# Up projections with features on partitions, two activation buffers, and modulation sums in pieces: one change to a two-block transformer kernel

## The chip, the cores and the metric

The kernel runs as one program on one core of a Trainium2 chip. A core has a matmul engine (TensorE, PE), three elementwise engines (VectorE or DVE, ScalarE or ACT, GpSimd or POOL), and SyncE (SP), which here only issues transfers from the chip's memory. The metric is the device time of one execution in microseconds (us), lower being better. A kernel's time is the median of its runs. Engines run their own instruction streams in program order and meet only at semaphores: an instruction waits until a counter has reached a value, and adds to a counter when it is done. So what stands ahead of an instruction on its engine delays it, whatever the data allow.

## The reference, cut to what matters

A two-layer block and then a one-layer block run over 256 tokens of 1024 features in float32. The parts that matter here:

```
def squared_relu_mlp(h, w_up, w_down):          # layers 0 and 1: D_FF = 4096
    a = jax.nn.relu(h @ w_up)
    return (a * a) @ w_down

for i in range(2):                              # first block
    mod = silu(c) @ w_mod[i] + b_mod[i]         # 1024 x 6144, a vector for each layer
    sh1, sc1, g1, sh2, sc2, g2 = split(mod, 6)
    y = pool_mixer(...) if i == 0 else moba_attention(...)
    x = x + g1 * y
    h = modulate(rmsnorm(x, norm_mlp[i]), sh2, sc2)
    x = x + g2 * squared_relu_mlp(h, w_up[i], w_down[i])

def swiglu(x, w_gate, w_up, w_down):            # second block: D_FF_2 = 2816
    return (silu(x @ w_gate) * (x @ w_up)) @ w_down
```

The second block has a gated delta rule and an attention with forgetting between its input projection and its SwiGLU; the change doesn't touch them.

## The kernel before, in words

**Precision.** Every large product is made of three passes in float32r: the high part of the weights (`wh`) by the high part of the data (`H`, or `aTh` for the activation), the low part of the weights (`wl`) by the high part of the data, and `wh` by the low part (`L`, `aTl`). The high part of a loaded weight block is a copy made by ScalarE (line 557), the low part a subtraction on VectorE (line 1049).

**Weights.** `raw` has four slots of 2 MB, loaded by SP. `wh` and `wl` hold one weight block at a time, in two halves. A block is called T; `split(T)` is four pieces, two for each half, first on ScalarE (which waits for the load, and for `split_used`, that TensorE has used the same half of the block before), then on VectorE (which waits for ScalarE's piece). TensorE waits with `half(T, hb)` for VectorE's second piece of a half. SP may load a slot again when VectorE has split the block in it (`free_split`).

**An MLP iteration.** Each of the first two MLPs has 8 iterations of 512 hidden features, numbered 0 to 7 and 8 to 15. `up(it)` makes 256 tokens x 512 features, tokens on partitions, in two banks of PSUM: for each half of the weights (4 of the 8 blocks of 128 input features) and each of 2 token blocks, 4 x 3 matmuls of 512 columns, 48 in all. ScalarE takes the relu of it (line 602), POOL squares it (line 452), `turn(it)` transposes it with 8 matmuls against the identity (line 1646) into two more banks, ScalarE copies out the high part `aTh` (line 607), VectorE the low part `aTl` (line 1083), and `down(it)` adds its product with 512 rows of `w_down` into four banks (line 1661, 48 matmuls). TensorE's order is up(0), turn(0), up(1), down(0), turn(1), up(2), down(1), turn(2) and so on: up(j), down(j - 1), turn(j). The T of up(j) in the first MLP is T_MLP0 - 1 + 2j, of down(j) T_MLP0 + 2 + 2j. The SwiGLU stage has 11 iterations of 256 features with the gate's and the up's columns side by side in one block (`g_up`, line 1593), a product on VectorE in place of the square (line 1489), four transposes (`g_turn`, line 2066) and 24 matmuls of `g_down` (line 2077).

**Modulation sums.** The vector `mod` needs 12 blocks of 512 columns for each layer. VectorE multiplies a block's rows by silu(c) and adds them up into `acc` (`mod_sum`, line 909), and TensorE sums over the partitions with one-column matmuls (line 1547, 1712, 1723). During the first MLP this goes on for layer 1: in iterations 2 to 7 a unit of 2 x 256 columns is loaded into slots 0 and 1, `mod_halves(j)` sums it on VectorE in one piece of 16 instructions (lines 933 and 936), TensorE's 8 small matmuls follow down(j - 1), and `mod_cols1(j)` adds the bias to the result in PSUM (line 964). Slots 0 and 1 are loaded again when `mod_halves` is done with them; the last block of `w_down` goes into slot 0 after unit 7. `gate_diag` and `gate_mm` (lines 993 and 1611) spread a gate over the partitions, by 8 small VectorE instructions and 16 matmuls, before the last down projection.

**Query and key projections.** They already have the other layout (line 1749): weights stationary, tokens moving, 256 columns a matmul, features on partitions.

The order of VectorE's work in the first MLP's loop, which the prediction follows:

```
with e.Fori(2, 7) as j:
    split(T_MLP0 + 2 * j, 3)          # down(j - 1)
    mod_halves(j)
    split(T_MLP0 + 1 + 2 * j, 2)      # up(j + 1)
    mod_cols1(j)
    mlp_aT(j)
```

## Time and profile before

| what | value |
|---|---|
| median of 3 runs | 1230.62 us (1228.77 to 1233.9) |
| span of the profiled execution | 1229.1 us |
| mean granted TensorE clock, share of 2.4 GHz | 0.892 |
| TensorE busy | 1098.8 us (89%), 5513 matmuls |
| VectorE busy | 681.5 us (55%) |
| ScalarE busy | 451.5 us (37%) |
| GpSimd busy | 109.6 us (9%) |
| data loaded | 193.76 MB, 159 GB/s over the span |

The span runs from the first to the last instruction of one profiled execution. It is the only time that this execution has of its own; it lies inside the range of the runs, 1.5 us below their median. Busy is time in which an engine had at least one instruction in work. A matmul's row gives a modelled length from its start until its last result (0.39 us for 512 columns), but matmuls are pipelined, so what counts is the distance between the starts of two neighbours. The first MLP lies at 114 to 323 us, the second at 516 to 712, the SwiGLU stage at 1017 to 1219.

### The profile page before, as it was taken

How to read it: one execution, taken by the hardware profiler on the slowest of the kernel's cores; microseconds unless marked ns; L12 is line 12 of the kernel's file. 1: busy time of each engine (PE TensorE's matmuls, PEld its weight loads, DVE VectorE, ACT ScalarE, POOL GpSimd, SP SyncE). 2: the span in 40 equal slices, each digit the busy share in tenths (PEclk: the TensorE clock that was granted, in tenths of full speed). 3: DMA queues.
4: the chain of work that ended last, by engine and by line, in shares of the span. 5: the costliest groups of instructions: out<-in, count | busy, mean ns of one | idle time of the engine just before them, and what ended most of it. 6: DMA issues, size and time to landing. Idle time of an engine off the chain costs nothing.

```text
span 1229.1 us, 14350 instructions
## 1 busy us (share of the span) xinstructions
PE 1098.8 (89%) x5513; PEld 927.8 (75%) x5513; DVE 681.5 (55%) x1074; ACT 451.5 (37%) x748; POOL 109.6 (9%) x108
## 2 busy tenths in 40 slices
PE   5489999999799898899999879999869689999995
PEld 5488777777698688678888669986659677777774
DVE  5487666776645894544444366623373545554453
ACT  1113433433444321444444345542222334443342
POOL 2000100101000000010010010001074000000000
PEclk9976999999799657899999869985679988999998
DMA  9876577677354653154454513540000023545510
GB/s 342 286 271 228 211 253 266 208 270 271 140 206 151 206 192 138 71 200 160 185 196 177 188 47 131 203 137 1 1 1 1 19 85 103 183 159 191 185 68 34
DMA packets 105178, 195.47 MB, mean 159 GB/s; under 512 B 2283, under 2 KB 46572, under 8 KB 105132
## 3 DMA queue, kind: packets, MB, share of 16 engines
q1 hardware_dynamic: 104380, 192.58, 44.6%
q0 software_dynamic: 752, 2.26, 0.5%
q8 instruction: 31, 0.51, 0.2%
q14 instruction: 15, 0.12, 0.0%
HBM read 193.76 MB, written 1.07 MB: 159 GB/s over the span
## 4 chain that ended last, share of the span: by engine, by line
PE 70%; DVE 16%; ACT 5%; issue 5%; DMA 3%; POOL 1%; SPq 1%; DVEq 0%; ACTq 0%; POOLq 0%
PE ps L1593 16%; PE ps L1632 12%; PE ps L1661 10%; PE ps L1858 6%; DVE wl L1049 5%; PE ps L1749 4%; DMA raw<-in_w_mod 3%; PE ps L2077 3%; DVE arena L909 2%; PE ps L1543 2%; ACT wh L557 2%; DVE arena L936 2%; PE ps L1993 1%; ACT arena L574 1%; PE ps L1762 1%
## 5 line engine op out<-in xcount | busy, mean ns | idle before, releaser
L1049 DVE TENSOR_TENSOR wl<-raw,wh 128x1024 fp32r<-128x1024 f32 (+1 forms) x288 | 314.0, 1135 | 306.1 <-ACT wh L557 305.8
L557 ACT ACTIVATE wh<-raw 128x1024 fp32r<-128x1024 f32 (+1 forms) x288 | 267.9, 982 | 364.6 <-PE ps L1593 135.1
L1593 PE MATMUL ps<-wh,H 128*128 128x512 f32 x288 | 117.5, 408 | 6.1 <-DVE L L1032 3.3
L1593 PE MATMUL ps<-wl,H 128*128 128x512 f32 x288 | 116.2, 403 | 0.0
L1593 PE MATMUL ps<-wh,L 128*128 128x512 f32 x288 | 115.4, 401 | 0.0
L1661 PE MATMUL ps<-wh,aTh 128*128 128x512 f32 x256 | 103.2, 403 | 8.9 <-DVE wl L1049 8.9
L1632 PE MATMUL ps<-wh,H 128*128 128x512 f32 x256 | 103.4, 404 | 2.4 <-DVE wl L1049 2.4
L1661 PE MATMUL ps<-wl,aTh 128*128 128x512 f32 x256 | 102.7, 401 | 0.0
L1661 PE MATMUL ps<-wh,aTl 128*128 128x512 f32 x256 | 102.5, 400 | 0.0
L1632 PE MATMUL ps<-wl,H 128*128 128x512 f32 x256 | 101.4, 396 | 0.0
L1632 PE MATMUL ps<-wh,L 128*128 128x512 f32 x256 | 101.2, 395 | 0.0
L452 POOL TENSOR_TENSOR arena<-arena 128x512 f32<-128x512 f32 x32 | 45.2, 1428 | 347.7 <-ACT arena L602 347.7
L1593 PEld LDWEIGHTS ps<-wh,H 128*128 128x128 f32 x288 | 55.9, 194 | 22.5 <-DVE wl L1049 5.0
L1593 PEld LDWEIGHTS ps<-wh,L 128*128 128x128 f32 x288 | 55.6, 193 | 13.2
L1661 PEld LDWEIGHTS ps<-wh,aTh 128*128 128x128 f32 x256 | 49.0, 191 | 21.6 <-issue 6.9
L1593 PEld LDWEIGHTS ps<-wl,H 128*128 128x128 f32 x288 | 55.7, 194 | 12.1
L1632 PEld LDWEIGHTS ps<-wh,H 128*128 128x128 f32 x256 | 48.7, 190 | 15.9 <-issue 3.9
L1661 PEld LDWEIGHTS ps<-wh,aTl 128*128 128x128 f32 x256 | 49.0, 191 | 12.1
L1661 PEld LDWEIGHTS ps<-wl,aTh 128*128 128x128 f32 x256 | 49.1, 192 | 11.9
L1632 PEld LDWEIGHTS ps<-wh,L 128*128 128x128 f32 x256 | 48.5, 189 | 11.6
L1858 PE MATMUL ps<-H,wh 128*128 128x272 f32 x192 | 56.8, 296 | 0.3 <-DVE wl L1049 0.3
L1858 PE MATMUL ps<-L,wh 128*128 128x272 f32 x192 | 56.4, 294 | 0.0
(373 smaller groups left out, 1943.2 us busy)
## 6 DMA issues: line engine op xcount, KB each, us to landing
raw<-in_w_up SPq DMA_DIRECT2D x16, 2048.0 KB, 7.5
raw<-in_w_down SPq DMA_DIRECT2D x16, 2048.0 KB, 7.7
raw<-in_w_mod SPq DMA_DIRECT2D x12, 2048.0 KB, 9.7
raw<-in_w_in SPq DMA_DIRECT2D x7, 2048.0 KB, 7.5
raw<-in_w_mod SPq DMA_DIRECT2D x12, 1024.0 KB, 7.5
raw<-in_w_qkv SPq DMA_DIRECT2D x6, 2048.0 KB, 10.9
raw<-in_w_mod SPq DMA_DIRECT2D x8, 1536.0 KB, 7.0
raw<-in_w_gate SPq DMA_DIRECT2D x11, 1024.0 KB, 5.3
```

The source lines that it names most:

```text
L452: e.tensor_tensor(act[:, m, :], relu[:, m, :], relu[:, m, :], ALU.mult).then_inc(S["a_done"], 1)
L557: e.activation(dst, src, ACT.Copy).then_inc(S["split_h"], 1)
L909: ins = e.scalar_tensor_tensor(out=dst, in0=w[:, k, :], scalar=ccol[:, 0, k:k + 1], in1=dst, op0=ALU.mult, op1=ALU.add)
L936: ins = e.scalar_tensor_tensor(out=dst, in0=w[:, k, 0:256], scalar=ccol[:, 0, k:k + 1], in1=dst, op0=ALU.mult, op1=ALU.add)
L1049: e.tensor_tensor(o, src, i1.bitcast(F32), ALU.subtract).then_inc(S["split_l"], 1)
L1543: e.matmul(ps[:, 2, c:c + 1], w[:, k, P * c:P * c + P], ccol[:, 0, k:k + 1], start=(c == 0 and k == 0), stop=False)
L1593: ins = e.matmul(ps[:, bank, :], src[xa][:, 4 * hb + k, META + P * m:META + P * m + P], w[wb][:, k, :], start=(hb == 0 and k == 0 and n == 0),
L1632: ins = e.matmul(ps[:, 4 + m, :], (H, L)[xa][:, 4 * hb + k, META + P * m:META + P * m + P], w[wb][:, k, :], start=(hb == 0 and k == 0 and ...
L1661: ins = e.matmul(ps[:, 2 * m + c, :], (aTh, aTl)[xa][:, 2 * hb + k, P * m:P * m + P], w[wb][:, k, 512 * c:512 * c + 512], start=False, sto ...
L1749: ins = e.matmul(ps[:, b + hb, SEQ * c:SEQ * c + SEQ], w[wb][:, k, P * c:P * c + P], (H, L)[xa][:, k, META:TT], start=(k == 0 and n == 0), ...
L1858: ins = e.matmul(ps[:, b + 2 * hb + c, 0:TT], w[wb][:, k, P * c:P * c + P], (H, L)[xa][:, k, :], start=(k == 0 and n == 0), stop=(k == KD ...
L2077: ins = e.matmul(ps[:, 2 * m + c, :], (aTh, aTl)[xa][:, hb, P * m:P * m + P], (wh, wl)[wb][:, hb, 512 * c:512 * c + 512], start=False, sto ...
```

## The change

Four edits, in all three MLP stages:

- The up projections take the layout of the key projections. `feature_rows` keeps 128 features of the weights stationary and moves the 256 tokens: 96 matmuls of 256 columns. Half b of the block now gives 256 finished features in bank 4 + b, and is split with `cols=True`. The result has its features on partitions, so `turn` and `g_turn` are gone.
- `aTh` and `aTl` have two buffers each. ScalarE takes the relu of a bank and squares it into `aTh` (`mlp_act`); VectorE squares the same relu in full precision and subtracts (`mlp_low`). POOL squares nothing. In SwiGLU VectorE multiplies once for all 256 tokens, ScalarE copies the high part, VectorE subtracts.
- `mod_halves` is called in pieces of one or more rows k (two instructions each) between the pieces of the splits. `acc` has two column ranges, used in turn; the small matmuls write bank 6. On TensorE the small matmuls of unit j stand between up(j + 1) and down(j), and `mod_cols1(j)` is the last thing of step j on VectorE. Unit 7 is cut in two, ahead of and behind `mlp_low(7)`; the gate diagonals and `mod_cols1(7)` follow the split of the last down block. `mod_sum(11)` moves between the two halves of up(2)'s split.
- On TensorE the order is up(0), up(1), down(0), up(2), small matmuls, down(1), up(3), small matmuls, down(2) and so on.

```diff
@@ -123,11 +123,11 @@
...
-relu = at("relu", 8, [P, NM, 512])
-act = at("act", 12, [P, NM, 512])
+act = at("act", 8, [P, 4, SEQ])
+relu = at("relu", 56, [P, 4, SEQ])
...
-aTh = nc.alloc_sbuf_tensor_at("aTh", [P, 4, SEQ], F32R, offset=arena_at + 16 * 1024)
-aTl = nc.alloc_sbuf_tensor_at("aTl", [P, 4, SEQ], F32R, offset=arena_at + 20 * 1024)
+aTh = [nc.alloc_sbuf_tensor_at(f"aTh{i}", [P, 4, SEQ], F32R, offset=arena_at + (12 + 8 * i) * 1024) for i in range(2)]
+aTl = [nc.alloc_sbuf_tensor_at(f"aTl{i}", [P, 4, SEQ], F32R, offset=arena_at + (16 + 8 * i) * 1024) for i in range(2)]
@@ -446,18 +446,8 @@
...
-    def squares(it):
-        for m in range(NM):
-            e.wait_ge(S["r_done"], 2 * it + m + 1)
-            e.tensor_tensor(act[:, m, :], relu[:, m, :], relu[:, m, :], ALU.mult).then_inc(S["a_done"], 1)
-    squares(0)
-    with e.Fori(1, 8) as j:
-        squares(j)
...
-    squares(8)
-    with e.Fori(9, 16) as j:
-        squares(j)
@@ -593,20 +583,15 @@
...
-    def mlp_relu(it, t):
-        for m in range(NM):
-            if m == 0:
-                e.wait_ge(S["u_done"], it + 1)
-            else:
-                e.wait_ge(S["split_used"], 2 * t + 2)
-            e.activation(relu[:, m, :], ps[:, 4 + m, :], ACT.Relu).then_inc(S["r_done"], 1)
-    def mlp_aT(it):
-        for b in range(2):
-            e.wait_ge(S["t_done"], 2 * it + b + 1)
-            e.activation(aTh[:, 2 * b:2 * b + 2, :],
-                         ps[:, 6 + b, :].rearrange("p (k t) -> p k t", k=2), ACT.Copy).then_inc(S["th_done"], 1)
+    def mlp_act(it, buf, t, b, first=False):
+        e.wait_ge(S["split_used"], 2 * t + b + 1)
+        if not first:
+            e.wait_ge(S["a_done"], 2 * it - 1 + b)
+        r = relu[:, 2 * b:2 * b + 2, :]
+        e.activation(r, ps[:, 4 + b, :].rearrange("p (k t) -> p k t", k=2), ACT.Relu).then_inc(S["r_done"], 1)
+        e.wait_ge(S["r_done"], 2 * it + b + 1)
+        e.activation(aTh[buf][:, 2 * b:2 * b + 2, :], r, ACT.Square).then_inc(S["th_done"], 1)
@@ -920,16 +908,16 @@
...
-    def mod_halves(j):
+    def mod_halves(j, r, ks):
...
-        for k in range(KD):
+        for k in ks:
...
-                w, dst = kview(hb), acc[:, hb, 0:256]
+                w, dst = kview(hb), acc[:, hb, 256 * r:256 * r + 256]
...
-                        e.wait_ge(S["mod_mm"], 10 + j)
+                        e.wait_ge(S["mod_mm"], 9 + j)
@@ -1077,11 +1065,17 @@
...
-    def mlp_aT(it):
+    def mlp_low(it, buf, first=False):
...
+            e.wait_ge(S["r_done"], 2 * it + b + 1)
+            if not first:
+                e.wait_ge(S["tl_done"], 2 * it - 1 + b)
+            r = relu[:, 2 * b:2 * b + 2, :]
+            e.tensor_tensor(act[:, 2 * b:2 * b + 2, :], r, r, ALU.mult).then_inc(S["a_done"], 1)
...
-            e.tensor_tensor(aTl[:, 2 * b:2 * b + 2, :], ps[:, 6 + b, :].rearrange("p (k t) -> p k t", k=2),
-                            aTh[:, 2 * b:2 * b + 2, :].bitcast(F32), ALU.subtract).then_inc(S["tl_done"], 1)
+            e.wait_ge(S["a_done"], 2 * it + b + 1)
+            e.tensor_tensor(aTl[buf][:, 2 * b:2 * b + 2, :], act[:, 2 * b:2 * b + 2, :],
+                            aTh[buf][:, 2 * b:2 * b + 2, :].bitcast(F32), ALU.subtract).then_inc(S["tl_done"], 1)
@@ -1142,34 +1136,47 @@
...
-    split(T_MLP0, landed(N_MLP0)[0])
+    split(T_MLP0, landed(N_MLP0)[0], cols=True)
...
-    split(T_MLP0 + 1, landed(14)[0], qs=(0, 1))
+    split(T_MLP0 + 1, landed(14)[0], cols=True)
+    mlp_low(0, 0, first=True)
+    split(T_MLP0 + 2, 3)
+    mlp_low(1, 1)
+    split(T_MLP0 + 3, 2, cols=True, qs=(0, 1))
...
-    split(T_MLP0 + 1, landed(14)[0], qs=(2, 3))
-    mlp_aT(0)
-    split(T_MLP0 + 2, 3)
-    split(T_MLP0 + 3, 2)
+    split(T_MLP0 + 3, 2, cols=True, qs=(2, 3))
...
-    e.tensor_tensor(modc[:, 0, 40:48], ps[:, 5, 0:8], pcol[:, 0, 40:48], ALU.add).then_inc(S["mod_col"], 2)
-    mlp_aT(1)
-    with e.Fori(2, 7) as j:
-        split(T_MLP0 + 2 * j, 3)
-        mod_halves(j)
-        split(T_MLP0 + 1 + 2 * j, 2)
+    e.tensor_tensor(modc[:, 0, 40:48], ps[:, 6, 0:8], pcol[:, 0, 40:48], ALU.add).then_inc(S["mod_col"], 2)
+    def mlp0_steps(j, r):
+        split(T_MLP0 + 2 * j, 3, qs=(0, 1))
+        mod_halves(j, r, (0, 1))
+        split(T_MLP0 + 2 * j, 3, qs=(2, 3))
+        mod_halves(j, r, (2, 3))
+        mlp_low(j, r)
+        split(T_MLP0 + 1 + 2 * j, 2, cols=True, qs=(0, 1))
+        mod_halves(j, r, (4, 5))
+        split(T_MLP0 + 1 + 2 * j, 2, cols=True, qs=(2, 3))
+        mod_halves(j, r, (6, 7))
         mod_cols1(j)
-        mlp_aT(j)
-    mod_halves(7)
+    with e.Fori(1, 3) as i:
+        for r in range(2):
+            mlp0_steps(2 * i + r, r)
+    mlp0_steps(6, 0)
+    split(T_MLP0 + 14, 3, qs=(0, 1))
+    mod_halves(7, 1, (0, 1, 2))
+    split(T_MLP0 + 14, 3, qs=(2, 3))
+    mlp_low(7, 1)
+    mod_halves(7, 1, (3, 4, 5, 6, 7))
+    split(T_MLP0 + 15, 0)
...
-    split(T_MLP0 + 14, 3)
     gate_diag(modc[:, 0, 40:48])
     mod_cols1(7)
-    mlp_aT(7)
-    split(T_MLP0 + 15, 0)
@@ -1479,36 +1487,42 @@
...
-    split(T_FFN, N_FFN % R, qs=(0, 1))
+    split(T_FFN, N_FFN % R, cols=True, qs=(0, 1))
...
-    split(T_FFN, N_FFN % R, qs=(2, 3))
-    def g_mul(j):
-        for m in range(NM):
-            e.wait_ge(S["gr_done"], 2 * j + m + 1)
-            e.tensor_tensor(act[:, m, 0:256], relu[:, m, 0:256], ps[:, 4 + m, 256:512], ALU.mult
-                            ).then_inc(S["ga_done"], 1)
-    def g_aT(j):
+    split(T_FFN, N_FFN % R, cols=True, qs=(2, 3))
+    def g_mul(j, t):
+        e.wait_ge(S["gr_done"], j + 1)
+        e.wait_ge(S["split_used"], 2 * t + 2)
+        if not (isinstance(j, int) and j == 0):
+            e.wait_ge(S["gtl_done"], j)
+        e.tensor_tensor(act[:, 0:2, :], relu[:, 0:2, :], ps[:, 5, :].rearrange("p (k t) -> p k t", k=2), ALU.mult
+                        ).then_inc(S["ga_done"], 1)
+    def g_low(j, buf):
...
-        e.tensor_tensor(aTl[:, 0:2, :], ps[:, 6, :].rearrange("p (k t) -> p k t", k=2),
-                        aTh[:, 0:2, :].bitcast(F32), ALU.subtract).then_inc(S["gtl_done"], 1)
-    split(T_FFN + 1, (N_FFN + 1) % R, qs=(0, 1))
-    g_mul(0)
-    split(T_FFN + 1, (N_FFN + 1) % R, qs=(2, 3))
-    g_aT(0)
+        e.tensor_tensor(aTl[buf][:, 0:2, :], act[:, 0:2, :], aTh[buf][:, 0:2, :].bitcast(F32), ALU.subtract
+                        ).then_inc(S["gtl_done"], 1)
+    split(T_FFN + 1, (N_FFN + 1) % R, cols=True, qs=(0, 1))
+    g_mul(0, T_FFN)
+    split(T_FFN + 1, (N_FFN + 1) % R, cols=True, qs=(2, 3))
+    g_low(0, 0)
...
-            split(T_FFN + 2 + 2 * r + 4 * i, (N_FFN + 2 + 2 * r) % R, words=HALF)
-            g_mul(1 + r + 2 * i)
+            j, t = 1 + r + 2 * i, T_FFN + 2 + 2 * r + 4 * i
+            split(t, (N_FFN + 2 + 2 * r) % R, words=HALF)
+            g_mul(j, t - 1)
...
-                split(T_FFN + 3 + 2 * r + 4 * i, (N_FFN + 3 + 2 * r) % R)
-            g_aT(1 + r + 2 * i)
+                split(t + 1, (N_FFN + 3 + 2 * r) % R, cols=True, qs=(0, 1))
+            g_low(j, 1 - r)
+            if not (last and r):
+                split(t + 1, (N_FFN + 3 + 2 * r) % R, cols=True, qs=(2, 3))
@@ -1616,39 +1630,28 @@
...
-    def up(it, t, mods_in=None):
-        for hb in range(2):
-            half(t, hb)
-            w = [q[:, hb, :].rearrange("p (k n) -> p k n", k=4) for q in (wh, wl)]
-            for m in range(NM):
-                if hb == 0 and not (isinstance(it, int) and it == 0):
-                    e.wait_ge(S["r_done"], 2 * it - 1 + m)
-                if hb == 0 and m == 1 and mods_in is not None:
-                    e.wait_ge(S["mod_col"], mods_in)
-                for k in range(4):
-                    parts(4 * hb + k)
+    def feature_rows(t, free):
+        for b in range(2):
+            half(t, b)
+            if free is not None:
+                e.wait_ge(free[0], free[1] + (b if len(free) == 3 else 0))
+            w = [q[:, b, :].rearrange("p (k n) -> p k n", k=KD) for q in (wh, wl)]
+            for c in range(2):
+                for k in range(KD):
+                    parts(k)
...
-                        ins = e.matmul(ps[:, 4 + m, :], (H, L)[xa][:, 4 * hb + k, META + P * m:META + P * m + P],
-                                       w[wb][:, k, :], start=(hb == 0 and k == 0 and n == 0),
-                                       stop=(hb == 1 and k == 3 and n == 2))
-                if hb == 1 and m == 0:
-                    ins.then_inc(S["u_done"], 1)
+                        ins = e.matmul(ps[:, 4 + b, SEQ * c:SEQ * c + SEQ], w[wb][:, k, P * c:P * c + P],
+                                       (H, L)[xa][:, k, META:TT], start=(k == 0 and n == 0),
+                                       stop=(k == KD - 1 and n == 2))
...
-    def turn(it):
-        e.wait_ge(S["a_done"], 2 * it + 2)
-        if not (isinstance(it, int) and it == 0):
-            e.wait_ge(S["tl_done"], 2 * it)
-        for k in range(4):
-            for m in range(NM):
-                ins = e.transpose(ps[:, 6 + k // 2, (k % 2) * SEQ + P * m:(k % 2) * SEQ + P * m + P],
-                                  act[:, m, P * k:P * k + P], ident[:, :])
-            if k % 2:
-                ins.then_inc(S["t_done"], 1)
-    def down(it, t, last=False):
+    def up(it, t):
+        first = isinstance(it, int) and it == 0
+        feature_rows(t, None if first else (S["r_done"], 2 * it - 1, "each half"))
+    def down(it, buf, t, last=False):
@@ -1702,31 +1705,40 @@
...
-    turn(0)
...
-    down(0, T_MLP0 + 2)
-    e.wait_ge(S["r_done"], 4)
+    down(0, 0, T_MLP0 + 2)
+    up(2, T_MLP0 + 3)
...
-        ins = e.matmul(ps[:, 5, c:c + 1], acc[:, c // 4, P * (c % 4):P * (c % 4) + P], ones[:, 0:1],
+        ins = e.matmul(ps[:, 6, c:c + 1], acc[:, c // 4, P * (c % 4):P * (c % 4) + P], ones[:, 0:1],
...
-    turn(1)
-    with e.Fori(2, 8) as j:
-        up(j, T_MLP0 - 1 + 2 * j, 10 + j)
-        down(j - 1, T_MLP0 + 2 * j)
-        e.wait_ge(S["r_done"], 2 * j + 2)
+    down(1, 1, T_MLP0 + 4)
+    def mods_layer1(j, r):
...
+        e.wait_ge(S["mod_col"], 10 + j)
...
-            ins = e.matmul(ps[:, 5, c:c + 1], acc[:, c // 2, P * (c % 2):P * (c % 2) + P], ones[:, 0:1],
-                           start=True, stop=True)
+            ins = e.matmul(ps[:, 6, c:c + 1], acc[:, c // 2, 256 * r + P * (c % 2):256 * r + P * (c % 2) + P],
+                           ones[:, 0:1], start=True, stop=True)
...
-        turn(j)
+    with e.Fori(1, 3) as i:
+        for r in range(2):
+            j = 2 * i + r
+            up(j + 1, T_MLP0 + 1 + 2 * j)
+            mods_layer1(j, r)
+            down(j, r, T_MLP0 + 2 + 2 * j)
+    up(7, T_MLP0 + 13)
+    mods_layer1(6, 0)
+    down(6, 0, T_MLP0 + 14)
+    mods_layer1(7, 1)
...
+    e.wait_ge(S["r_done"], 16)
...
-    down(7, T_MLP0 + 15, last=True)
+    down(7, 1, T_MLP0 + 15, last=True)
...
```

Left out of the diff: the same calls in the second MLP (`mlp_act`, `mlp_low`, `mlp_steps` without modulation sums), ScalarE's side of SwiGLU, the buffer index in `down` and `g_down`, and the removal of `g_turn`.

## Rows read from the trace of the kernel before

**Rows 1.** The page: shares of the chain that ended last; ScalarE's high pieces (mean ns).
```profile
PE 70%; DVE 16%; ACT 5%; issue 5%; DMA 3%; POOL 1%; SPq 1%; DVEq 0%; ACTq 0%; POOLq 0%
...
L557 ACT ACTIVATE wh<-raw 128x1024 fp32r<-128x1024 f32 (+1 forms) x288 | 267.9, 982 | 364.6 <-PE ps L1593 135.1
```

**Rows 2.** The chain in order of time, MLP stages: start us, length us, what.
```profile
554.84 11.12 PE ps L1632 x48
565.96 11.20 PE ps L1661 x48
578.03 11.13 PE ps L1632 x48
...
1049.33 11.39 PE ps L1593 x48
...
1067.06 11.39 PE ps L1593 x48
```

**Rows 3.** Timeline of PE, key projections: start us, modelled length us.
```profile
339.86 0.28 PE L1749 MATMUL ps<-H,wh 128*128 128x256 f32 x1
...
342.94 0.28 PE L1749 MATMUL ps<-L,wh 128*128 128x256 f32 x1
```

**Rows 4.** Timeline of PE, first MLP: start us, us, idle before and its releaser.
```profile
127.21 1.10 PE L1646 MATMUL ps<-ident,arena 128*128 128x128 f32 x8 [1.95 <-POOL arena L452]
...
134.75 0.50 PE L1632 MATMUL ps<-wh,H 128*128 128x512 f32 x1 [0.88 <-DVE wl L1049]
...
226.61 1.02 PE L1723 MATMUL ps<-ones,arena 128*128 128x1 f32 x8
...
228.87 0.50 PE L1632 MATMUL ps<-wh,H 128*128 128x512 f32 x1 [0.30 <-DVE wl L1049]
```

**Rows 5.** Timeline of DVE in one iteration of the first MLP.
```profile
218.74 2.18 DVE L933 TENSOR_SCALAR arena<-raw,ccol 128x256 f32<-128x256 f32 x2
220.84 5.62 DVE L936 SCALAR_TENSOR_TENSOR arena<-raw,ccol,arena 128x256 f32<-128x256 f32 x14
226.39 4.62 DVE L1049 TENSOR_TENSOR wl<-raw,wh 128x1024 fp32r<-128x1024 f32 x4
```

**Rows 6.** Groups by line and shape on DVE: busy us, mean ns of one.
```profile
L909 DVE SCALAR_TENSOR_TENSOR arena<-raw,ccol,arena 128x512 f32<-128x512 f32 x58 | 44.3, 763 | 2.1
...
L993 DVE TENSOR_SCALAR arena<-ident,mods 128x128 f32<-128x128 f32 x8 | 1.7, 281 | 0.0
...
L1378 DVE TENSOR_TENSOR junk<-k_t 128x512 f32<-128x512 f32 x2 | 1.4, 680 | 0.0
```

**Rows 7.** Timeline of PE, waits before the first MLP's last two down projections.
```profile
292.43 0.50 PE L1661 MATMUL ps<-wh,aTh 128*128 128x512 f32 x1 [2.34 <-DVE wl L1049]
...
309.79 0.47 PE L1661 MATMUL ps<-wh,aTh 128*128 128x512 f32 x1 [2.39 <-DVE wl L1049]
```

**Rows 8.** Timeline of SP, first MLP's end: when the last down load is issued.
```profile
289.74 0.38 SPq L266 DMA_DIRECT2D raw<-in_w_down  x1
```

**Rows 9.** DMA issues between 250 and 310 us: KB each, median us to landing.
```profile
raw<-in_w_down SPq DMA_DIRECT2D x2, 2048.0 KB, 7.8
```

**Rows 10.** Timeline of PE, second MLP: its first wait and its last.
```profile
530.56 1.09 PE L1646 MATMUL ps<-ident,arena 128*128 128x128 f32 x8 [1.80 <-POOL arena L452]
...
698.17 0.76 PE L1661 MATMUL ps<-wh,aTh 128*128 128x512 f32 x1 [4.17 <-DVE wl L1049]
...
703.84 0.39 PE L1661 MATMUL ps<-wl,aTh 128*128 128x512 f32 x1
```

**Rows 11.** Windows: us, PE, PEld, DVE, ACT, POOL busy, PEclk as share of 2.4 GHz.
```profile
294.00:296.00 2.00, 2.00 (x10) 1.62 (x9) 2.00 (x3) 0.00 (x0) 2.00 (x2) 1.00 1.02 420
313.00:315.00 2.00, 2.00 (x7) 1.59 (x6) 0.18 (x2) 0.00 (x0) 0.00 (x0) 0.58 0.96 255
```

**Rows 12.** Timeline of PE, the last wait of the SwiGLU stage.
```profile
1211.37 0.47 PE L2077 MATMUL ps<-wh,aTh 128*128 128x512 f32 x1 [2.70 <-DVE wl L1049]
...
1216.02 0.39 PE L2077 MATMUL ps<-wl,aTh 128*128 128x512 f32 x1
```

143 lines of the change are left out of this document (64 added, 79 removed).

## The prediction

> **What bounds the kernel now.** I read the page's chain first: TensorE holds most of it, and nothing else comes near [rows 1]. So the three MLP stages were read next in the chain's order of time. In the second MLP it is TensorE without a break: 48 matmuls of an up projection in 11.12 us, 48 of a down projection in 11.20, and the next up 0.87 us after that, which is the eight transposes of the turn [rows 2]. In the SwiGLU stage the up projection restarts every 17.73 us [rows 2]. In the first MLP there is more between down and up: eight one-column matmuls (1.02 us), eight transposes, and 0.30 us of waiting for VectorE's low-half splits (L1049), together 2.5 us from the end of the down's stream, 0.24 before 226.61, to 228.87 [rows 4]. VectorE is why: the modulation sums of one unit stand in one piece of 16 instructions before those splits [rows 5]. A reader should see that the transposes lie in full on the path, and that three real waits stand at stage ends: before the first MLP's last downs [rows 7], the second's [rows 10] and SwiGLU's [rows 12]. All of TensorE's waits on the splits, ACT's included, follow one pattern: a half of the weight buffer is released, ScalarE writes two high pieces (1.0 each, [rows 1]), VectorE two low ones, and TensorE meanwhile has the other half.
>
> **Up projections.** Each turns from 48 matmuls of 512 columns into 96 of 256. The same loop already runs in the key projections: 27 rows from 339.86 to 342.94, so 26 intervals of 0.1185 us [rows 3]. 96 x 0.1185 = 11.37 against 11.12, so 0.25 us dearer each, 16 + 11 times: 6.7 us in all, counted inside the stages below. Bounds: nothing (the columns are the same) and 0.5 us (twice it), 0 to 13 us in all. Of the fixed cost there is a rule in the Trainium skill, TensorE: Matmul & The Clock Gate, section Back-to-back issue gap: columns at 2.4 GHz plus 2.5 ns for each. It would make each up only 0.12 us dearer and the sum 3.5 us lower; the row disagrees and is used.
>
> **Second MLP.** The turns go. At its first turn stand a wait of 1.80 [rows 10] and the eight transposes with what hands over to them, some 1.0: 2.8 us. Six steady turns of 0.87 are 5.2. At the end down(14) is followed by transposes (1.0) and a wait of 4.17, to 698.17: 5.2 us. After that wait 13 matmuls take 5.67 us (698.17 to 703.84) where at 0.233 they would take 3.03, the granted clock's lower level, 1.2 GHz, by their doubled spacing [rows 10]: 2.6 us. All of it goes if nothing takes its place. What must now be ready: for down(j) the low activations, four VectorE instructions (two squares at 0.68 [rows 6], two subtractions like them, 2.7 us), issued between the splits of the down and of the next up. Counted from the release of up(j)'s second half, ScalarE needs 2.2 us and VectorE ends its two splits at about 3.6; mlp_low ends at 6.2, the release of the down's first half is at 5.6, its high piece is there at 6.8, the low pair at 9.2, and TensorE wants it at 11.2. Hidden with 2 us to spare; without that cover it would cost what it is late. Sum: 2.8 + 5.2 + 5.2 + 2.6 - 8 x 0.25 = 13.8 us gained. POOL's squares leave the path with the turn.
>
> **First MLP, the steady part.** Here the added order bites. On TensorE the one-column matmuls now stand between up(j+1) and down(j). On VectorE mod_cols1(j), which waits for them, stands ahead of the low split of down(j)'s first half. ScalarE's high pieces are ready, but VectorE sits in that wait through all of up(j+1), and behind it queue two low pieces that TensorE needs at once. So before each down: 0.24 us to the one-column matmuls and 1.02 for them [rows 4], 0.15 for handing over and the tiny add, two pieces at 4.62 / 4 = 1.16 [rows 5]: 3.75 us, of which about 2.5 is idle. Gone is the 2.5 us between down and up. Net for an iteration: 3.75 + 0.25 - 2.5 = 1.5, over the five iterations from down(1) to down(6) 7.5 us, less the wait of 2.34 before down(6) [rows 7], which the same stall replaces: 5.2 us lost. The sums in pieces are themselves hidden: VectorE has 9.3 us of splits, 6 of sums and 2.7 of mlp_low in a step of 26 us. Bounds: -7 (VectorE's wait somehow covered: 2.5 x 5 less) and +8.
>
> The two tensor_scalars of a sum took 2.18 us while POOL squared [rows 5]; the Trainium skill, SBUF — State Buffer, says of the port pair that VectorE and GpSimd share that the loser waits for the whole instruction. They should shrink to some 0.7 us. This is VectorE time off the path, worth nothing here.
>
> **First MLP, start.** Turn(0) goes: 3.0 us around the wait of 1.95, and the wait of 0.88 before up(1)'s second half [rows 4]. Against it: the first 24 matmuls of up(0) now need all eight feature pairs, about 0.9 us late; 2 x 0.25; and mod_sum(11), eight instructions at up to 0.763 [rows 6], moves between the two splits of up(2) and makes it about 0.6 us late; the sixteen one-column matmuls meet the same stall as above (4.6 us in place of 2.7). 3.9 - 0.9 - 0.5 - 0.6 - 0.25 - 1.9: nothing, within 2 us.
>
> **First MLP, end.** Before, down(6) starts at 292.43 and down(7) at 309.79 [rows 7], with a granted clock of 0.58 of full from 313 to 315 [rows 11], for which I take the 1.6 us priced below, it ends 12.8 us later: 30.2 us from down(6)'s start. The last down weights share slot 0 with the modulation unit, so SP issues their load only when its sum is done, at 289.74 [rows 8], 2.7 us ahead of down(6). Now ten of the sixteen sum instructions come after mlp_low(7). From down(6)'s start: six of them 2.2, two splits 2.3, mlp_low 2.6, up to slot 0's last 3.6 (0.40 each, [rows 5]): issue at 10.8. Landing 7.8 later [rows 9]: 18.6. ScalarE's first piece 1.1, four low pieces 4.6: 24.3. Only behind them stand the eight gate diagonals, 1.7 [rows 6], and the add without which TensorE doesn't start the gate matmuls (2 to 2.8 us): 28.5. Then down(7) cold, 11.2 + 2.6: 42.3. Loss 12.1 us. Bounds by the landing (5 to 11 us): 9 to 15.
>
> **Clock.** The five stalls in the steady part leave TensorE nearly idle for some 2.5 us after the small matmuls. A wait of 2.34 kept full clock, 1.00 in the window behind it; 2.39 was followed by 0.58, and 2.70 and 4.17 by doubled spacings [rows 7, 10, 11, 12]. The price at 2.70: 13 matmuls in 4.65 in place of 3.03, 1.6 us [rows 12]. The stall lies at the edge, so I take three of five: 4.8 us; bounds 0 and 13 (five at 2.6).
>
> **SwiGLU.** Before the last down 0.6 of transposes, 2.70 of wait and 1.6 of clock go [rows 12]: 4.9. The first turn gives about 1 us (estimate from the same rows, without the wait). In the ten steady steps the gap before each up isn't the transposes but the splits: from the release of the down's first half 3.5 us are needed and the second half gives 2.8; they stay late by 0.7, so removing the turn buys nothing and each up costs its 0.25, of which half may hide: 1 us lost. Gain 4.9, within 2.
>
> **Sum.** 5.2 + 12.1 + 4.8 - 13.8 - 4.9 = +3.4 us. The profiled execution has a span of 1229.1; the median of the runs is 1230.6, 1.5 above. 1230.6 + 3.4 = 1234.0.
>
> **The rivals.** (1) The clock falls after every stall, at the larger price: 13 in place of 4.8, 1242. For it: the small matmuls leave the array almost unused, so the quiet stretch is 3.75 us; against it: the wait of 2.34 passed unharmed [rows 11]. The same page of the Trainium skill, HAM oscillation, warns of exactly a wait in each tile that makes each next burst start slow. (2) VectorE's wait is not exposed: if the add returned before up(j+1) ends, the two pieces would be ready. Then 12.5 and 4.8 go: 1217, faster. It decides from half of the stall hidden; the order of the waits in the code speaks against it. (3) The end of the first MLP isn't paid, the load landing behind down(6): 1222. It would need the slot free 8 us sooner. (4) Narrow matmuls at 0.5 us a projection: +6.7, 1241. (5) The change does nothing that shows: gains and losses as above but smaller, 1231.
>
> **How the numbers follow.** Forecast with (5) 0.48, (1) 0.25, (2) 0.13, (3) 0.09, (4) 0.05. 0.5% is 6.2 us, about what these runs can tell from no change: faster is below 1224.5, slower above 1236.8. Faster: (2) and half of (3), 0.17. Slower: (1), (4), less a sixth of them, and 0.08 of the forecast's own upper side, 0.33. Same 0.50. The range leaves out (2) and the far side of (1): 1221 to 1243; the likeliest case alone 1228 to 1240.
>
> **What would show it.** Second MLP: a period of 22.6 us, no wait before down(15), end about 13.8 us nearer to its start. First MLP: steps of 26.3 us or more, TensorE idle some 2.5 us before each down, released by VectorE's low pieces, VectorE idle before the add of mod_cols1; 10 to 14 us of TensorE idle before the last gate matmuls; clock windows at 0.5 after some stalls. SwiGLU: the same 17.8 us period. Wrong would be: steps of 24 us in the first MLP, a new wait in the second, or 256-column matmuls off 0.118.

## The result, and the profile after

The changed kernel takes 1243.1 us (median of 4 runs, 1240.7 to 1244.3); the kernel before, run beside it, takes 1231.2 us (4 runs, 1228.8 to 1233.9). The ratio is 1.0108, with a 95% interval of 1.0069 to 1.0146: slower by about 1%. The forecast was 1234.0 in a range of 1221 to 1243. Slower by over 0.5% had been given a chance of 0.33, and the time lies just past the range's upper end. The profiled execution has a span of 1239.0 us against 1229.1, so the traces have to account for +9.9 us, where the sum said +3.4. That is 6.5 of the 9.1 us by which the forecast was off. The other 2.6 aren't in the traces: the profiled execution was the shortest of the four (1240.7 us), and its span lies 4.1 us below their median, where the forecast took the 1.5 us of the kernel before.

First the page of the changed kernel: busy times, the chain's shares, and two groups of instructions (busy us, mean ns of one | idle before them).

```profile
PE 1087.9 (88%) x6637; PEld 976.6 (79%) x6637; DVE 695.9 (56%) x1095; ACT 455.5 (37%) x737; POOL 60.3 (5%) x76
...
PE 75%; DVE 14%; ACT 4%; DMA 3%; issue 3%; POOL 1%; SPq 1%; DVEq 0%; ACTq 0%
...
L1644 PE MATMUL ps<-H,wh 128*128 128x256 f32 x864 | 245.6, 284 | 9.8 <-DVE wl L1037 7.9
...
L1664 PE MATMUL ps<-wh,aTh 128*128 128x512 f32 x256 | 106.9, 418 | 17.1 <-DVE wl L1037 17.1
```

TensorE's share of the chain has risen from 70% [rows 1] to 75%. The second number of the last two rows is modelled length, not spacing, so it isn't the price of a narrow matmul; that is read off the chain. What the page does say is where TensorE waits: 17.1 us ahead of down projections (L1664), all on VectorE's low pieces.

The chain in order of time gives the stages. The second MLP and then the SwiGLU stage, start us, length us, what:

```profile
573.91 11.33 PE ps L1644 x96
585.24 11.20 PE ps L1664 x48
...
697.91 18.21 PE ps L1664 x78
...
1059.01 1.09 issue
1060.10 1.23 DVE wl L1037
1061.45 11.59 PE ps L1644 x96
1073.04 2.81 PE ps L2072 x12
1077.02 1.09 issue
1078.11 1.23 DVE wl L1037
1079.47 11.61 PE ps L1644 x96
```

The second MLP has no wait left: up 11.33, down 11.20, a period of 22.53 us, and the last two downs run on as one piece. From its first up (538.05) to the next stage (741.58) it takes 203.5 us against 217.8 before: 14.2 gained. SwiGLU has a period of 18.02 us against 17.73 [rows 2], and the reader should see the two pieces between the first half of a down and the next up: "issue" and one low piece, which TensorE waits out for the last 0.8 us.

The first MLP is where it is lost. The starts of down(2) and down(5) on TensorE, with the idle time before them; then VectorE ahead of the first of these:

```profile
193.51 0.60 PE L1664 MATMUL ps<-wh,aTh 128*128 128x512 f32 x1 [2.75 <-DVE wl L1037]
...
278.65 0.50 PE L1664 MATMUL ps<-wh,aTh 128*128 128x512 f32 x1 [3.13 <-DVE wl L1037]
```

```profile
190.93 0.16 DVE L952 TENSOR_TENSOR modc<-ps,pcol 128x4 f32 x1 [7.23 <-PE ps L1725]
191.09 2.36 DVE L1037 TENSOR_TENSOR wl<-raw,wh 128x1024 fp32r<-128x1024 f32 x2
```

VectorE stands idle for 7.23 us in front of a 0.16 us addition (L952, mod_cols1), and is released by TensorE's small column sums (L1725). Only then come the two low pieces (L1037) that down(2) needs, and TensorE waits 2.75 us for them. All six downs from down(1) to down(6) have such a gap, of 2.6 to 3.1 us. The first 3 us behind two of the gaps, as windows (length, then busy time of PE, PEld, DVE, ACT and POOL, then the granted clock):

```profile
193.50:196.50 3.00, 2.99 (x8) 2.34 (x9) 3.00 (x6) 0.00 (x0) 0.00 (x0) 0.54 0.99 363
249.30:252.30 3.00, 3.00 (x7) 2.44 (x8) 3.00 (x6) 0.00 (x0) 0.00 (x0) 0.50 0.95 349
```

The lower level, 1.2 GHz, reads 0.50, so these stretches lie wholly or nearly so in it. The same window stands at 0.50 to 0.57 behind each of the six gaps.

Last the end of this stage: SP's issue of the last w_down, ScalarE's high pieces, VectorE, and TensorE, one view after another:

```profile
316.99 0.38 SPq L266 DMA_DIRECT2D raw<-in_w_down  x1
```

```profile
324.59 3.90 ACT L547 ACTIVATE wh<-raw 128x1024 fp32r<-128x1024 f32 x4 [18.37 <-DMA raw<-in_w_down]
```

```profile
325.68 4.63 DVE L1037 TENSOR_TENSOR wl<-raw,wh 128x1024 fp32r<-128x1024 f32 x4 [8.32 <-ACT wh L547]
330.23 1.65 DVE L981 TENSOR_SCALAR arena<-ident,modc 128x128 f32<-128x128 f32 x8
331.80 0.15 DVE L952 TENSOR_TENSOR modc<-ps,pcol 128x4 f32<-128x4 f32 x1
```

```profile
332.00 3.78 PE L1625 MATMUL ps<-arena,ones 128*128 128x128 f32 x16 [11.86 <-DVE modc L952]
335.44 0.78 PE L1664 MATMUL ps<-wh,aTh 128*128 128x512 f32 x1
```

Down(6) starts at 306.37. The load is issued 10.6 us later and landed 7.6 after that; behind the four low pieces stand the diagonals (L981) and the addition (L952), and TensorE is idle for 11.86 us until the gate's matmuls. Down(7) ends at 347.7, 41.3 us after down(6)'s start. The forecast said 10.8, 7.8 and 42.3.

Two stages that the change doesn't touch differ too. From 356.82 to 538.05 (the query, key and value projections and the attention of the first block) the changed kernel is 2.5 us shorter. Most of it is one projection, in the chain of the kernel before and then of the changed one:

```profile
480.90 21.26 PE ps L1593 x84
```

```profile
504.84 19.70 PE ps L1607 x84
```

Its first 3 us ran at a granted clock of 0.66 in the kernel before and of 1.00 in the changed one, and the gate's 16 matmuls ahead of it take 1.8 us in place of 2.8. In a3_end_order, a variant of the changed kernel, the same projection takes 21.3 us again, at 0.50. So this is the level at which the clock stood there in one execution, and no gain of the change.

From 741.58 to 1029.05 (the third stage: input projection, attention and delta rule of the second block) the changed kernel is 4.1 us longer. That has one place, on VectorE (L1404, which is L1396 of the kernel before), among ten products of 128 or 16 x 512 elements; `Kb` is one of them, and GpSimd works beside it on seven of its own:

```profile
903.10 6.76 DVE L1404 TENSOR_TENSOR Kb<-k_t,coef 128x512 f32<-128x512 f32 x1
```

```profile
903.29 2.03 POOL L489 TENSOR_TENSOR arena<-v_t,beta 128x512 f32<-128x512 f32 x2
905.29 1.03 POOL L490 TENSOR_TENSOR R1m<-kv_m,beta 16x512 f32<-16x512 f32 x1
```

The kernel before, the same stretch, VectorE and then GpSimd:

```profile
894.84 1.53 DVE L1396 TENSOR_TENSOR Kb<-k_t,coef 128x512 f32<-128x512 f32 x1
```

```profile
894.32 2.95 POOL L499 TENSOR_TENSOR arena<-v_t,beta 128x512 f32<-128x512 f32 x2
...
901.57 3.88 POOL L504 TENSOR_TENSOR arena<-k_t,coef 128x512 f32<-128x512 f32 x1
```

One multiplication takes 6.76 us in place of 1.53, while six of GpSimd's products run at 1.03 us each. In the kernel before both paid: GpSimd up to 3.88 us for one product, VectorE 1.52 or 1.53 for each of five. From the first Kn's start to the second Qg's end VectorE's ten products take 14.6 us in place of 10.3.

### The profile page after: what moved, and what is told of

It reads as the page before. It is cut to its first block, busy times and chain, and to the rows that moved or that the text cites. A ratio compares the mean times of both kernels' runs of the same rounds, so it can differ in the third digit from the quotient of the medians.

```text
span 1239.0 us, 16571 instructions
## 1 busy us (share of the span) xinstructions
PE 1087.9 (88%) x6637; PEld 976.6 (79%) x6637; DVE 695.9 (56%) x1095; ACT 455.5 (37%) x737; POOL 60.3 (5%) x76
## 4 chain that ended last, share of the span: by engine, by line
PE 75%; DVE 14%; ACT 4%; DMA 3%; issue 3%; POOL 1%; SPq 1%; DVEq 0%; ACTq 0%
PE ps L1644 25%; PE ps L1664 13%; PE ps L1867 6%; PE ps L1607 5%; DVE wl L1037 4%; PE ps L1761 4%; PE ps L2072 3%; DMA raw<-in_w_mod 2%; PE ps L1557 2%; DVE arena L897 1%; ACT wh L547 1%; PE ps L2002 1%; ACT arena L564 1%; PE ps L1774 1%; PE ps L1799 1%
## 5 line engine op out<-in xcount | busy, mean ns | idle before, releaser
L1037 DVE TENSOR_TENSOR wl<-raw,wh 128x1024 fp32r<-128x1024 f32 (+1 forms) x288 | 313.8, 1132 | 280.2 <-ACT wh L547 280.1
L1644 PE MATMUL ps<-H,wh 128*128 128x256 f32 x864 | 245.6, 284 | 9.8 <-DVE wl L1037 7.9
L1644 PE MATMUL ps<-H,wl 128*128 128x256 f32 x864 | 244.6, 283 | 0.0
L1644 PE MATMUL ps<-L,wh 128*128 128x256 f32 x864 | 244.2, 283 | 0.0
L1644 PEld LDWEIGHTS ps<-H,wh 128*128 128x128 f32 x864 | 165.0, 191 | 17.5 <-issue 14.4
L1644 PEld LDWEIGHTS ps<-L,wh 128*128 128x128 f32 x864 | 165.2, 191 | 0.0
L1644 PEld LDWEIGHTS ps<-H,wl 128*128 128x128 f32 x864 | 164.3, 190 | 0.5
L1664 PE MATMUL ps<-wh,aTh 128*128 128x512 f32 x256 | 106.9, 418 | 17.1 <-DVE wl L1037 17.1
L1664 PE MATMUL ps<-wl,aTh 128*128 128x512 f32 x256 | 105.8, 413 | 0.0
L1664 PE MATMUL ps<-wh,aTl 128*128 128x512 f32 x256 | 105.3, 411 | 0.0
L1664 PEld LDWEIGHTS ps<-wh,aTh 128*128 128x128 f32 x256 | 51.2, 200 | 29.5 <-DVE wl L1037 12.0
L1664 PEld LDWEIGHTS ps<-wh,aTl 128*128 128x128 f32 x256 | 50.9, 199 | 12.7
L1664 PEld LDWEIGHTS ps<-wl,aTh 128*128 128x128 f32 x256 | 51.1, 199 | 11.9
L1867 PE MATMUL ps<-H,wl 128*128 128x272 f32 x192 | 56.3, 293 | 0.0
L1557 PE MATMUL ps<-ccol,raw 128*128 128x1 f32 x208 | 39.5, 322 | 15.8 <-DVE modc L908 15.8
L1607 PE MATMUL ps<-wh,H 128*128 128x512 f32 x112 | 45.6, 408 | 2.7 <-DVE L L1020 2.7
L1607 PE MATMUL ps<-wl,H 128*128 128x512 f32 x112 | 45.2, 404 | 0.0
## 6 DMA issues: line engine op xcount, KB each, us to landing
raw<-in_w_qkv SPq DMA_DIRECT2D x6, 2048.0 KB, 14.2
```

Source lines behind the costliest of these rows:

```text
L1037: e.tensor_tensor(o, src, i1.bitcast(F32), ALU.subtract).then_inc(S["split_l"], 1)
L1557: e.matmul(ps[:, 2, c:c + 1], w[:, k, P * c:P * c + P], ccol[:, 0, k:k + 1], start=(c == 0 and k == 0), stop=False)
L1607: ins = e.matmul(ps[:, bank, :], src[xa][:, 4 * hb + k, META + P * m:META + P * m + P], w[wb][:, k, :], start=(hb == 0 and k == 0 and n == 0),
L1644: ins = e.matmul(ps[:, 4 + b, SEQ * c:SEQ * c + SEQ], w[wb][:, k, P * c:P * c + P], (H, L)[xa][:, k, META:TT], start=(k == 0 and n == 0), ...
L1664: ins = e.matmul(ps[:, 2 * m + c, :], (aTh, aTl)[xa][buf][:, 2 * hb + k, P * m:P * m + P], w[wb][:, k, 512 * c:512 * c + 512], start=False ...
L1867: ins = e.matmul(ps[:, b + 2 * hb + c, 0:TT], w[wb][:, k, P * c:P * c + P], (H, L)[xa][:, k, :], start=(k == 0 and n == 0), stop=(k == KD ...
```

## The experiments

The kernel before was run beside every group: 1229.5 (24 runs), 1228.6 (7) and 1229.6 us (18). All kernels but two (c1 and c3) are built on the changed one, 1243.1 us.

**a1_late_cols: the addition behind the low pieces.** In VectorE's step of unit j:

```diff
 split(T_MLP0 + 2 * j, 3, qs=(0, 1))
 mod_halves(j, r, (0, 1))
 split(T_MLP0 + 2 * j, 3, qs=(2, 3))
+if cols: mod_cols1(j - 1)
 ...
 mod_halves(j, r, (6, 7))
-mod_cols1(j)
```

> The changed kernel, with VectorE's addition of the modulation columns of unit j moved behind its low pieces of both halves of the next w_down tile (mod_cols1(j) now follows split(T_MLP0 + 2(j+1)) instead of preceding it). Theory A, that this wait is what opens the gap before every down: the gaps of 2.5 to 3.1 us before down(2) to down(6) are gone, TensorE's granted clock stays at 1.00 from the second step on, the downs take 11.2 us instead of 12.7 to 14.2, a step of the first MLP takes 23 to 24 us instead of 28.4, and the time falls by 5 x 5 = 25 us to 1216 to 1222. Theory B, that the gap belongs to ScalarE's high pieces or to the weights' transfers, which the columns' addition only happens to cover: the gap stays within 0.5 us, with another releaser, and the time stays within 3 us of 1243. Theory C, that only the last of several late things goes: the gap halves, but the clock still falls in each, and the time falls by 5 to 10 us.

Measured: 1223.9 us (1222.2 to 1226.8), ratio to before 0.9972 (0.9947 to 0.9998). Down(2) on TensorE and the end's gate matmuls, then the window behind down(2):

```profile
191.19 0.48 PE L1666 MATMUL ps<-wh,aTh 128*128 128x512 f32 x1
...
312.70 3.79 PE L1627 MATMUL ps<-arena,ones 128*128 128x128 f32 x16 [13.94 <-DVE modc L952]
```

```profile
191.20:194.20 3.00, 3.00 (x15) 2.45 (x15) 1.87 (x4) 2.57 (x4) 0.00 (x0) 1.00 1.06 382
```

There is no idle time before down(2) to down(6), and in the 3 us behind each of these starts the granted clock reads 1.00. Steps take 23.6 us in place of 28.3. This is Theory A, though 19 us came and not 21 to 27, and the time lies just outside the 1216 to 1222 expected: down(1)'s gap wasn't touched, so four full steps and one in part gained (20.8 us up to down(6)), and the wait at the end grew from 11.86 to 13.94 us.

**a2_fill_gap: the stall kept, the array kept busy.** On TensorE, between the small column sums and down(2) to down(6), with bank 7 as a target that nobody reads:

```diff
 mods_layer1(j, r)
+for _n in range(20):
+    e.matmul(ps[:, 7, 0:SEQ], H[:, 0, META:META + P], H[:, 1, META:TT], start=True, stop=True)
 down(j, r, T_MLP0 + 2 + 2 * j)
```

> The changed kernel with 20 more matmuls of 256 columns on TensorE (a result nobody reads, in PSUM bank 7) between the small column sums and the wait of down(2) to down(6). They take 20 x 0.118 = 2.4 us, which is time that TensorE stands idle in now. If the long downs (12.7 to 14.2 us instead of 11.2) come from the clock that falls after each idle gap: the granted clock stays at 1.00, each of the five downs takes 11.2 to 11.5 us, and the time falls by 8 to 11 us to 1232 to 1235, though no wait has been removed. If they come from anything else (ports, transfers, instruction supply): the downs keep their length and the time is 1243 to 1246.

Measured: 1235.3 us (1234.0 to 1237.8), ratio 1.0052 (1.0030 to 1.0073). Down(3), and the window behind down(2):

```profile
220.49 0.50 PE L1664 MATMUL ps<-wh,aTh 128*128 128x512 f32 x1 [0.64 <-DVE wl L1037]
```

```profile
193.90:196.90 3.00, 3.00 (x13) 2.45 (x14) 3.00 (x6) 0.00 (x0) 0.00 (x0) 1.00 0.97 356
```

TensorE still waits for VectorE, now 0.2 to 0.8 us behind the filler, but the clock is 1.00 behind all five and in 3 us it begins 13 matmuls instead of 8. The time is 7.8 us below the changed kernel's, where 8 to 11 were expected. A step takes 26.5 us (193.89 to 299.70 in four). So of the 28.2 us of these steps in the changed kernel, 26.5 are work and stall and 1.8 are clock. The forecast of the stall without the clock was 26.3.

**a3_end_order: the end in another order.** VectorE, then TensorE:

```diff
 mod_halves(7, 1, (3, 4, 5, 6, 7))
+gate_diag(modc[:, 0, 40:48])
 split(T_MLP0 + 15, 0)
-gate_diag(modc[:, 0, 40:48])
 mod_cols1(7)
...
-mods_layer1(7, 1)
-e.wait_ge(S["mod_col"], 18)
 e.wait_ge(S["r_done"], 16)
 gate_mm(4)
+mods_layer1(7, 1)
 down(7, 1, T_MLP0 + 15, last=True)
+e.wait_ge(S["mod_col"], 18)
```

> The changed kernel with the end of the first MLP in another order: on VectorE the eight gate diagonals stand ahead of the low pieces of the last w_down tile, on TensorE the gate's matmuls stand ahead of the column sums of unit 7, and the wait for unit 7's columns stands behind down(7). The last w_down tile still waits for the sum of unit 7. Down(7) is then released by its own low pieces: it starts some 6 to 7 us earlier in relation to down(6) (29.1 us between them now, 22 to 24 then), and the time is 1236 to 1238. If instead the diagonals and the gate were covered by the low pieces of the last tile already: less than 2 us.

Measured: 1239.4 us (1238.5 to 1241.1), ratio 1.0081 (1.0055 to 1.0106): 3.7 us less, and not the 5 to 7 expected. Down(7) starts 22.1 us after down(6) instead of 29.1, as expected, but it starts cold, with the gate's work no longer in the wait: its rows begin at 329.91 and the next stage at 352.95, which is 5.3 us nearer to down(6) than in the changed kernel. Behind 352.95 its profile is 2.0 us longer than the changed kernel's, in a place that neither edit touches: the projection ahead of the second MLP and the gate's matmuls before it, at the lower clock again.

**a4_cols_end: both orders**, the edits of a1 and a3 together.

> Both changes of order together (the columns' addition late, and the end in the new order). If the two are independent the savings add: 25 + 6 = 31 us, 1209 to 1216. If the end is bound by the chain sum of unit 6, transfer of unit 7's weights, sum of unit 7, transfer and split of the last w_down tile, then faster steps ahead of it run into that chain, and a part of the saving of the steps comes back as a longer stall ahead of down(7): 1214 to 1220.

Measured: 1219.0 us (1205.4 to 1221.2), ratio 0.9896 (0.9856 to 0.9935). From down(6)'s start to the QKV stage 46.0 us, against 45.2 in a3 and 50.5 in the changed kernel: the steps' saving comes through nearly whole, and the end still waits. The two savings add up (1243.1 - 19.2 - 3.7 = 1220.2). The 1214 to 1220 of the second expectation were met, but not by what it says: down(7) starts 22.8 us after down(6) against 22.1 in a3, so 0.7 us came back, and what was too large was the 31 us, summed from expectations that a1 and a3 had each missed.

**b1_slot: the last w_down tile issued earlier.** a4 with, on SP (VectorE reads unit 7's first half from slot 2):

```diff
+free_split(T_MLP0 + 13)
+e.dma_start(kview(2)[:, :, 0:256], wmod[1][:, :, 2560:2816]).then_inc(S["m7_in"], 16)
+e.wait_ge(S["mod_accb"], 6)
+load_mod1(1, slice(2816, 3072))
+e.wait_ge(S["mod_acc"], 16)
+for k in range(2):
+    load(0, dview(0)[:, 2 * k:2 * k + 2, :], wdn[0][7][:, 2 * k:2 * k + 2, :])
-e.wait_ge(S["mod_acc"], 17)
-load(0, dview(0), wdn[0][7])
```

> a4_cols_end with another slot for one transfer: the first half of unit 7's modulation weights goes into slot 2 (free as soon as up(7)'s tile has been split), so that the last w_down tile goes into slot 0 as soon as the sum of unit 6 has read it, instead of waiting for the sum of unit 7. In a4_cols_end TensorE stands idle for 7.7 us before down(7), which then takes 14.0 us at the fallen clock instead of 11.4. Theory A, that the transfer behind the sum of unit 7 sets this end: the idle time falls to 0 to 3 us, down(7) takes 11.4 to 13 us, and the time falls by 6 to 10 us from 1219 to 1209 to 1213. Theory B, that VectorE's own order (the sum of unit 7 and the diagonals stand ahead of the low pieces) sets it whatever the transfer does: the idle time stays above 5 us and the time within 3 us of 1219.

Measured: 1209.8 us (1208.1 to 1210.8), ratio 0.9852 (0.9809 to 0.9895), 9.2 less than a4. SP's issue in a4 and TensorE's wait before down(7) in it, then SP and the same wait in b1:

```profile
298.84 0.38 SPq L266 DMA_DIRECT2D raw<-in_w_down  x1
```

```profile
310.03 0.77 PE L1666 MATMUL ps<-wh,aTh 128*128 128x512 f32 x1 [7.66 <-DVE wl L1037]
```

```profile
280.10 0.37 SPq L326 DMA_DIRECT2D raw<-in_w_mod  x1
281.68 0.37 SPq L266 DMA_DIRECT2D raw<-in_w_mod  x1
282.09 1.34 SPq L266 DMA_DIRECT2D raw<-in_w_down  x2
```

```profile
303.93 0.47 PE L1677 MATMUL ps<-wh,aTh 128*128 128x512 f32 x1 [0.83 <-DVE wl L1048]
```

The load leaves 6.4 us before down(6) starts (288.50) and not 11.6 after it (287.20), and the wait falls from 7.66 to 0.83 us. Theory A holds: the slot was the end's limit. From down(6)'s start to the QKV stage it now takes 36.1 us; the kernel before took 39.5.

**b2_port: GpSimd waits for VectorE.** a4 with:

```diff
 e.wait_ge(S["coef_d"], 3)
+e.wait_ge(S["sc_d"], 10)
 for m in range(NM):
     e.tensor_tensor(R1[:, m], ...)
```

> a4_cols_end with one wait more on GpSimd in the third stage: its seven products R1, R1m, Kdm, R2, Kd start only when VectorE's ten products Kn to Qg are done. In the changed kernel, and in all four variants run so far, VectorE's Kb of 128x512 takes 6.76 us while GpSimd's products run beside it; in the kernel before it takes 1.53 us and GpSimd's own are the slow ones (up to 3.88 us). If the two engines slow each other: all ten of VectorE's take 0.67 us, GpSimd's take 1.03 us, TensorE gets Kb some 6 us earlier, and the time falls by 3 to 6 us to 1213 to 1216. If GpSimd's products are wanted at once by the work behind them: what is won at Kb is lost there, and the time is 1219 to 1222. If the 6.76 us come from elsewhere (an instruction fetched late), Kb stays at 6 us or more.

Measured: 1202.5 us (1195.5 to 1211.9), ratio 0.9817 (0.9741 to 0.9892). VectorE's Kb and GpSimd's first product:

```profile
866.72 0.78 DVE L1407 TENSOR_TENSOR Kb<-k_t,coef 128x512 f32<-128x512 f32 x1
```

```profile
872.48 2.04 POOL L490 TENSOR_TENSOR arena<-v_t,beta 128x512 f32<-128x512 f32 x2 [5.53 <-DVE Qg L1407]
```

Kb takes 0.78 us, VectorE's ten products together 6.9, GpSimd's 1.03 each, though they start later. The size can't be read off the median: in this profile the attention heads ahead of these products, which no edit touches, ran 12.9 us shorter at a higher granted clock (last section), and the four runs lie from 1195.5 to 1211.9. It can be read behind the heads: from the start of their last row reduction (841.11) to SwiGLU's first up projection (984.20) it takes 143.1 us, in a4 151.8 (855.81 to 1007.56). That is 8.7 us, more than the 3 to 6 expected; 0.6 of it is given back by SwiGLU's first up projection, 14.15 us in place of 13.57.

**b3_first: down(1)'s gap as well.** a4, and on VectorE:

```diff
 split(T_MLP0 + 3, 2, cols=True, qs=(2, 3))
-e.wait_ge(S["mod_mm"], 12)
-e.tensor_tensor(modc[:, 0, 40:48], ps[:, 6, 0:8], pcol[:, 0, 40:48], ALU.add).then_inc(S["mod_col"], 2)
 ...
 split(T_MLP0 + 4, 3, qs=(2, 3))
+(the same two lines)
```

> a4_cols_end with the gap before down(1) taken away in the same way as the others: VectorE's addition of the last eight columns of layer 0 stands behind its low pieces of both halves of down(1)'s tile. The gap is 2.7 us, and down(1) takes 13.6 to 14.0 us at the fallen clock instead of 11.4. If it is the same mechanism: the gap and the fallen clock go, 4 to 5.5 us less, 1214 to 1215. If down(1) also waits for its high pieces or for w_down's transfer: 0 to 2 us less.

Measured: 1213.7 us (1212.1 to 1214.9), ratio 0.9882 (0.9838 to 0.9925): 5.3 us less than a4, the same mechanism at its upper price. Down(1) stands in the trace without an idle time, its first 3 us at a granted clock of 1.00, and takes 11.3 us in place of 14.0:

```profile
162.74 0.48 PE L1667 MATMUL ps<-wh,aTh 128*128 128x512 f32 x1
```

**b4_all: the edits of a1, a3, b1, b2 and b3 together.**

> All of it: late columns in all six steps, the end's new order, the last w_down tile in slot 0 early, and GpSimd's wait. If the savings are independent they add up to 1219 - 8 - 4 - 5 = 1202, range 1198 to 1207. If the faster start of the first MLP only runs into the transfers (2 MB each of w_up, w_down and modulation weights in a step of 23.6 us, 267 GB/s where 356 GB/s is the most that the profile shows), a part comes back as gaps before ups and downs whose releaser is ScalarE behind a DMA: 1205 to 1212.

Measured: 1196.7 us (1194.9 to 1196.8), ratio 0.9742 (0.9700 to 0.9784). That is just below the 1198 to 1207 expected. The savings add; with the larger one of GpSimd's wait they come to what was measured (1219.0 - 9.2 - 8.7 - 5.3 = 1195.8). Here the heads ran at the low clock as in a4, so the wait can be read without taking anything out: 143.5 us from their last reduction to SwiGLU, 8.3 less than in a4. The 356 GB/s that the expectation calls the most is too low, since a stretch of the kernel before moved 420 [rows 11]; none of the gaps that it warns of shows in the time.

**c1_first_undone: the change without its first MLP.** The kernel before, with the changed layout in the second MLP and in SwiGLU alone. On TensorE, against the kernel before:

```diff
-turn(8)
 with e.Fori(0, 3) as i:
     for r in range(2):
-        up(9 + 2 * i + r, T_MLP1 + 1 + 4 * i + 2 * r)
-        down(8 + 2 * i + r, T_MLP1 + 2 + 4 * i + 2 * r)
-        turn(9 + 2 * i + r)
+        up_n(9 + 2 * i + r, T_MLP1 + 1 + 4 * i + 2 * r)
+        down_n(8 + 2 * i + r, r, T_MLP1 + 2 + 4 * i + 2 * r)
```

> The kernel before with the change made in the second MLP and in the SwiGLU alone; the first MLP, its modulation sums, its transposes and GpSimd's squares are as before. If the first MLP is what made the changed kernel slower: the time falls below the kernel before by what the traces show for the two other stages, 14.2 + 2.3 = 16.5 us, to 1212 to 1215; with VectorE's Kb at 6.76 us instead of 1.53 us, 4 us more, 1216 to 1219. If the 14.2 us of the second MLP were partly made by what the changed first MLP leaves behind (its clock, its loads), the time stays above 1222.

Measured: 1216.2 us (1215.3 to 1218.6), ratio 0.9897 (0.9881 to 0.9914). The chain, at the second MLP's first steady step, the stage behind it, and SwiGLU's start:

```profile
548.96 11.33 PE ps L1667 x96
...
716.63 38.82 PE ps L1930 x288
...
1004.18 13.58 PE ps L1667 x96
```

The second MLP (513.02 to 716.63) takes 203.6 us, as in the changed kernel. The stretch from 716.63 to 1004.18 is again 4.1 us longer than before, with Kb again at 6.76 us, though the first MLP is the old one. So without its first MLP the change gains 13.4 us, the third stage's loss included and with the projection ahead of the second MLP at the higher clock in the profile (19.7 us); the time lies in the 1216 to 1219 expected with a slow Kb. The first MLP costs 27 us on top (1243.1 - 1216.2), 24.8 by the two spans.

**c2_quarter: finer waits in SwiGLU.**

```diff
-half(t, b)
+e.wait_ge(S["split_l"], 4 * t + 2 * b + 1)
 ...
 for k in range(KD):
+    if c == 0 and k == 4:
+        half(t, b)
```

> The changed kernel, with finer waits in the SwiGLU's up projections alone: the first half of a tile starts when the first of its two low pieces is written (the matmuls of k 0 to 3), and waits for the second piece only ahead of k 4. Of the ten steps of 18.02 us some 1.1 us is TensorE waiting for the second piece, and a piece takes VectorE 1.2 us, while the twelve matmuls of k 0 to 3 take 1.4 us. If that wait is what the step is longer by than 11.4 + 5.6 us of matmuls: 16.9 to 17.1 us a step and 9 to 11 us less in all, 1232 to 1234. If TensorE waits there for the first piece too (ScalarE's high pieces behind g_down's first half): half of it, 3 to 6 us less. If the 1.1 us is something else (the issue of the matmuls): no change.

Measured: 1234.3 us (1231.1 to 1235.8), ratio 1.0035 (1.0009 to 1.0062), 8.8 us less than the changed kernel, at the lower edge of the 9 to 11 expected. The chain:

```profile
1063.98 11.36 PE ps L1649 x96
1075.33 5.60 PE ps L2077 x24
1080.93 11.31 PE ps L1649 x96
```

"issue" and the low piece are gone, and the period is 16.95 us instead of 18.02. TensorE waited for the second low piece of the first half, as supposed; the first was there. The SwiGLU stage, to the end of the span, is 9.8 us shorter in the profile.

**c3_before_port: GpSimd's wait in the kernel before**, the edit of b2 alone.

> The kernel before, with GpSimd's wait of b2_port alone. There VectorE's Kb takes 1.53 us and GpSimd's slowest product 3.88 us. If in this kernel too both engines pay for running beside each other: VectorE's ten products take 0.67 us each, and the time falls by 3 to 6 us, to 1224 to 1227. If the kernel before is the lucky order, in which GpSimd alone pays and nobody waits for it: within 1.5 us of 1229.5.

Measured: 1225.9 us (1216.6 to 1227.6), ratio 0.9967 (0.9948 to 0.9986). Kb:

```profile
886.06 0.69 DVE L1397 TENSOR_TENSOR Kb<-k_t,coef 128x512 f32<-128x512 f32 x1
```

The kernel before paid too. The medians differ by 3.7 us, in the expected range, but this kernel's runs mix the two speeds of the heads as well. Behind the heads its profile takes 143.6 us to SwiGLU, the kernel before 147.9 and the changed one 151.8: the wait is worth 4.3 us here and 8.3 there.

**c4_best: b4_all with c2's waits.**

> b4_all with the finer waits of c2_quarter: 1196.7 less the 9 to 11 us of the SwiGLU, 1186 to 1188, if nothing else in those steps (ScalarE's pieces, the transfers of 3 MB in 17 us) becomes the limit; 1190 to 1194 if only a part of it comes through.

Measured: 1185.0 us (1183.0 to 1187.5), ratio 0.9641 (0.9624 to 0.9658), 11.7 us less than b4_all and a little more than expected: 3.6% faster than the kernel before, 4.7% faster than the changed one.

## Why the prediction was wrong, and where right

The mechanisms were those forecast. The cost of the clock was sized too small and the gain of SwiGLU too large, and two differences stood in no term, one of them a cost. In spans, where forecast and trace stand side by side:

| term | forecast | measured | by |
|---|---|---|---|
| second MLP | -13.8 | -14.2 | chain; alone in c1 |
| first MLP, start, to down(1) | 0 | -0.4 | 164.98 against 165.34 |
| first MLP, steady, the stall | +5.2 | +4.9 | down(1) to down(6): 141.4 against 127.1, less the clock |
| clock behind the stalls | +4.8 | +9.4 | changed kernel less a2 (7.1), down(1) 13.65 against 11.32 in b3 (2.3) |
| first MLP, end of down(7) | +12.1 | +11.0 | 41.3 against 30.3 |
| SwiGLU | -4.9 | -2.3 | chain |
| QKV and attention | 0 | -2.5 | chain |
| third stage | 0 | +4.1 | Kb, b2, c1 |

The measured column adds up to 10.0; the spans differ by 9.9. The time missed the range by 0.1 us. With the clock's 4.6 us at their forecast it would have stayed inside, and so it would without the third stage's 4.1, which no term had; the profiled execution alone, 1240.7 us, lies inside as it is.

**Second MLP: right**, by its parts: period 22.53 for 22.6, no wait before down(15), and 11.33 for an up projection of 96 narrow matmuls where 11.37 was worked out from 0.1185 [rows 3]. The Trainium skill's formula for the gap (TensorE: Matmul & The Clock Gate, Back-to-back issue gap) gives 10.5 us for 96 such matmuls, and 11.2 if only its 2.5 ns for each further matmul are added to the 11.12 of the rows, as the forecast did. The trace stays with the row.

**First MLP, steady part: right.** Rival (2), that VectorE's wait isn't exposed, is refuted by the 7.23 us of idle time in front of the addition and by a1, which moves the addition behind the low pieces and so wins the stall back.

**The end: right** in its chain and nearly in its sum. The bound was 9 to 15. a3 and b1 take it apart: 5 us are the order behind the load, 9 the slot. Together that is more than the loss, and the end of b1 is shorter than that of the kernel before.

**The clock is the step that failed.** The forecast took "three of five" stalls to lower the clock, on the ground that a wait of 2.34 us kept it [rows 7, 11]. It fell behind every one of them. That was the condition of rival (1), given 0.25, but not its price: it said 2.6 us for each and 13 in all, where 1.9 and 9.4 were measured, and its 1242 us lie close to the result in part by luck, since the third stage lost 4.1 us too. Rows 7 and 11 were read by the length of the wait alone, and the reason against that was in the text: ahead of each new wait stand small one-column matmuls. The kernel before had shown the difference. Up to its wait of 2.34 us before down(6), after which the clock stayed at 1.00, wide matmuls run. Ahead of its wait of 2.39 us before down(7), after which it fell, TensorE did this (the eight transposes of the turn stand between the two rows):

```profile
303.73 0.95 PE L1723 MATMUL ps<-ones,arena 128*128 128x1 f32 x8
...
305.45 1.95 PE L1611 MATMUL ps<-arena,ones 128*128 128x128 f32 x16
```

Transposes stand ahead of the waits of 2.70 and 4.17 us as well. a2 shows that the price belongs to this stretch without wide matmuls and not to the late start: with down(j) as late as before and wide matmuls in the gap, the clock stays at 1.00. In a1 the small matmuls stand alone, without a wait, and it stays there too. How much of each it takes, no run tells. The price was 9.4 us in down(1) to down(5), or 1.9 each, within the bounds of 0 and 13. The Trainium skill (TensorE: Matmul & The Clock Gate, HAM oscillation) describes a wait in each tile, there for a transfer, behind which the next matmuls start slow. The trace agrees as to the pattern: it was so behind all six gaps, at 0.50 to 0.57.

**SwiGLU: the gain sized too large.** The text said that the splits and not the turn set the gap before each up, and that half of the dearer narrow matmuls would hide behind it. Nothing hid: the gap stayed, and from up(1) to up(10) 2.9 us were lost where 1 was forecast. The first turn gave 0.6 us instead of 1, the end 4.6 instead of 4.9.

**The third stage: not foreseen.** The change moves no instruction in it. VectorE and GpSimd run ten and seven products beside each other there, and how they hold each other up differs between the kernel before and the variants: Kb was at 6.76 or 6.77 us in the profiles of nine different kernels, the changed one and all variants of it or of its parts without GpSimd's wait, and at 1.53 in the kernel before. Taking GpSimd's work out from beside it removed the cost in both (143.1 to 143.6 us behind the heads in b2, b4 and c3). The Trainium skill (SBUF — State Buffer, SBUF: two separate sides) says that the engine that starts first holds the shared pair for its whole instruction while the other blocks. The trace shows more, and in part otherwise: one VectorE instruction was held through six of GpSimd's in a row, though its row starts 0.19 us ahead of the first of them. In the kernel before Kb's row starts 0.52 us behind GpSimd's first product, and there it took 1.53. So what differs is which of the two comes first, by some tenths of a microsecond. Whether that is what decides remains open; no run here varied it alone.

**The QKV and attention stage: no effect of the change.** Its -2.5 us are the clock in the projection and in the gate's matmuls ahead of the second MLP. In the profiles this projection takes either 19.7 us (changed kernel, a2, b1, b2, c1, c2, c4) or 21.3 (kernel before, a1, a3, a4, b3, b4, c3), whatever was edited. So +9.9 would have been about 12 with both at one level, and the -2.5 hid a part of the forecast's miss.

## What to carry to other kernels

When small results are passed back from TensorE to VectorE in a pipeline, the read of them is a wait on VectorE, and everything that feeds TensorE next must stand ahead of it: one addition of 0.16 us in the wrong place cost 19 us here. A stall of 2.5 to 3 us behind one-column matmuls is priced with the clock behind it, here 1.9 us for each; filling the gap with idle matmuls gives the clock back, removing the gap gives both. When two uses share a buffer slot, trace the last load of the stage through every use that comes before it: here a free slot next to it was worth 9 us, and waiting on the first quarter of a tile instead of the half 9 us more.

## What the runs showed that was not expected

The attention heads of the third stage run at two speeds in the same instruction stream. Windows of 8 us in a4_cols_end and in b2_port (columns as above):

```profile
824.00:832.00 8.00, 8.00 (x27) 5.65 (x24) 1.79 (x6) 1.80 (x8) 0.00 (x0) 0.50 0.00 0
```

```profile
824.00:832.00 8.00, 8.00 (x48) 6.30 (x48) 2.47 (x10) 2.82 (x11) 0.00 (x0) 1.00 0.01 2
```

At a granted clock of 0.50 the sixteen heads' row reductions take 35.9 us from first to last; where the clock came up, 23.0. In c3_before_port the first to the last took 28.4, and 35.9 in all the other profiles. The times of the kernel before, which reach from 1220.5 to 1234.1 us, have the spread that this would give, though only one of its executions was traced. So one profile of each kernel can differ by 12.9 us for a reason outside the change, and spans were compared here only where the heads took the same time. The projection ahead of the second MLP is a second such place, worth 1.6 us.

VectorE and GpSimd beside each other cost 8.3 us in one order and 4.3 in the other, by a single wait of GpSimd on VectorE, with no work removed.

A projection of 256-column matmuls costs 0.21 us more than one of 512 (11.33 against 11.12 [rows 2]) in the second MLP, where nothing waits.
